# A two-layer trunk with a hierarchical mixture of experts: further blocks taken apart, a third late expert, fillers between routing products

## What is computed

```python
def hierarchical_moe(t, wg, bg, we, be, w1, w3, w2):
    g_sel = jnp.argmax(g_logit, axis=-1)                       # 4 groups
    e_logit = jnp.take_along_axis(e_logit, g_sel[:, None, None], axis=1)[:, 0]
    top_p, top_i = lax.top_k(jax.nn.softmax(e_logit, axis=-1), TOP_K)     # 2 of 8
    top_w = top_p / jnp.sum(top_p, axis=-1, keepdims=True) * g_w
    ...
        hidden = jax.nn.silu(t @ w1_e) * (t @ w3_e)            # 1024 -> 256
        return acc + c_e[:, None] * (hidden @ w2_e), None      # for 32 experts
```

## Time and profile before

| | us |
|---|---|
| median of 3 runs (1046.13 to 1048.80) | 1048.57 |
| the profiled execution | 1048.56 |
| its span | 1046.8 |
| TensorE busy | 970.4 (93%) |
| VectorE / ScalarE / GpSimd busy | 362.8 / 248.2 / 213.4 |
| HBM read / written | 315.38 MB / 22.31 MB |

### The profile page before, as it was taken

One profiled execution on the slowest core, in us unless ns is written; L12 is line 12 of the kernel. 1 busy time (PEld: TensorE's weight loads), 2 busy tenths in 40 slices (PEclk: granted clock), 3 DMA queues, 4 the chain that ended last, 5 costly groups with the idle time before them and its releaser, 6 DMA issues.

```text
span 1046.8 us, 17807 instructions
## 1 busy us (share of the span) xinstructions
PE 970.4 (93%) x6151; PEld 614.8 (59%) x6152; DVE 362.8 (35%) x851; ACT 248.2 (24%) x537; POOL 213.4 (20%) x307
## 2 busy tenths in 40 slices
PE   5999999998998899998989899999998999998896
PEld 3444457545887455555555384877875555555552
DVE  4159493564337111110011370145444222221124
ACT  5110003444334122221221240033132111111112
POOL 1009300110001243332331100000003333333310
PEclk9999999999998899998999999999998999999899
DMA  9984546999715699999999899273646997999996
GB/s 361 307 273 176 198 115 233 315 339 381 293 66 191 228 385 406 406 406 407 407 406 406 320 317 309 81 279 108 223 166 232 389 399 290 407 405 403 404 405 232
DMA packets 129161, 315.95 MB, mean 302 GB/s; under 512 B 28969, under 2 KB 59969, under 8 KB 129076
## 3 DMA queue, kind: packets, MB, share of 16 engines
q1 hardware_dynamic: 113200, 295.98, 75.9%
q0 software_dynamic: 10880, 12.72, 3.6%
q10 hardware_dynamic: 4996, 6.09, 1.6%
HBM read 315.38 MB, written 22.31 MB: 323 GB/s over the span
## 4 chain that ended last, share of the span: by engine, by line
PE 73%; DMA 14%; DVE 5%; issue 3%; SPq 2%; ACT 2%; POOL 0%; POOLq 0%; DVEq 0%
PE ps L1095 17%; PE ps L929 16%; DMA ring<-in_moe_w 9%; PE ps L981 8%; PE ps L1121 8%; PE ps L939 5%; PE ps L883 3%; PE ps L1067 3%; SPq L699 2%; DMA ring<-in_w_mod 1%; PE ps L1248 1%; PE ps L1105 1%; DMA pair_out<-RH,sidx_all 1%; DMA RH<-hrow,sidx_all 1%; PE ps L896 1%
## 5 line engine op out<-in xcount | busy, mean ns | idle before, releaser
L1095 PE MATMUL ps<-ring,RT 128*64 128x256 f32 x2128 | 261.2, 399 | 26.2 <-DMA ring<-in_moe_w 22.6
L1095 PEld LDWEIGHTS ps<-ring,RT 128*64 128x64 f32 x2128 | 164.0, 143 | 98.6 <-issue 29.5
L929 PE MATMUL ps<-RT,ring 128*128 128x512 f32 (+1 forms) x544 | 182.0, 493 | 0.5 <-DVE RT L2244 0.5
L929 PEld LDWEIGHTS ps<-RT,ring 128*128 128x128 f32 x544 | 102.2, 190 | 76.5 <-issue 69.8
L2131 DVE TENSOR_TENSOR RT<-RT,ps 64x256 f32<-64x256 f32 x64 | 27.1, 423 | 275.7 <-ACT RT L1678 275.7
L1121 PE MATMUL ps<-ring,RT 128*64 128x512 f32 x424 | 100.4, 593 | 1.4 <-DVE RT L2137 1.0
L1678 ACT ACTIVATE RT<-ps 64x256 f32<-64x256 f32 x64 | 24.1, 377 | 254.0 <-PE ps L1095 254.0
L2286 DVE SCALAR_TENSOR_TENSOR RAB<-RM,chan,RAB 128x512 f32<-128x512 f32 x120 | 79.7, 746 | 0.0
L2535 POOL DMA_INDIRECT pair_out<-RH,sidx_all x62 | 63.2, 1019 | 54.0 <-POOL sidx_all L2532 54.0
L2511 POOL DMA_INDIRECT RH<-hrow,idx x8 | 8.4, 1046 | 308.5 <-DVE idx L2083 306.7
L2523 POOL DMA_INDIRECT RH<-hrow,sidx_all x56 | 59.0, 1054 | 50.8 <-POOL sidx_all L2520 48.1
(11 more groups left out here) (271 smaller groups left out, 1005.6 us busy)
## 6 DMA issues: line engine op xcount, KB each, us to landing
ring<-in_moe_w SPq DMA_DIRECT2D x358, 512.0 KB, 14.6
ring<-in_w_mod SPq DMA_DIRECT2D x96, 512.0 KB, 9.2
ring<-in_odd_w_in SPq DMA_DIRECT2D x24, 512.0 KB, 9.4
ring<-in_even_w_in SPq DMA_DIRECT2D x20, 512.0 KB, 9.5
ring<-in_even_w_out SPq DMA_DIRECT2D x8, 512.0 KB, 11.4
RAB<-in_moe_w SPq DMA_DIRECT2D x8, 512.0 KB, 7.9
RAB<-pair_out SPq DMA_DIRECT2D x8, 512.0 KB, 5.8
ring<-in_odd_w_out SPq DMA_DIRECT2D x8, 512.0 KB, 3.9
```

The lines of the kernel that those rows point to most:

```text
L929: mm = pe.matmul(bank, w[:, c, P * ft:P * (ft + 1)], moving[:, c, :], start=(c == 0), stop=(c == NCH - 1))
L1095: mm = pe.matmul(bank[CAP * k:CAP * (k + 1), 0:BLK], xt(c), w[k][:, BLK * c:BLK * (c + 1)], start=(c == 0), stop=(c == NCH - 1))
```

## The change

1. TensorE's step is now U(q), the further block's transposes and up products (`more_up`), Dn(q-1), Hd(q), the block's hidden and down products (`more_down`), T(q+2). Only the last further block of an expert is taken apart so; earlier ones of the same expert run whole, in a loop. ScalarE and VectorE follow the same split.
2. `LATE` has three experts. The zeroing moves from before step 0 to before step 28, with `XG[:, 0]` as source. The late rows have three buffers of their own (`XG[:, 0]`, `YS[:, 0]`, `YS[:, 1]`), and the one-hot products of the late experts are interleaved with Dn(31). Their slots are transposed tile by tile, in steps 28 and 29.
3. The choice of two goes by `dve.max` (the eight largest) on the logits and on keys that also hold the expert's place, one tile at a time; tile 0's group choice is a shorter chain.
4. One `warm` product pair between any two blocks of `slot_rows`; in layer 1 eight behind them instead of four; in layer 0 one tile's row transposes take the place of `warm(("lgT", l, 0), 3)`.

```diff
-LATE = (EXPERTS - 2, EXPERTS - 1)
+LATE = (EXPERTS - 3, EXPERTS - 2, EXPERTS - 1)
...
                 mm = rows(out, at_slot[:, (b + 1) % 2, :, :], vs)
                 if b < n_blocks - 2:
                     mm.then_inc(slot_used, 1)
+                if b == 0:
+                    drained(pe, "rank", l)
+                if b < n_blocks - 1:
+                    warm(("rank", l), 1)
...
-                def step(i, q, count, ahead=True):
-
-                    if ahead:
-                        T(*job_after(i, q, 1))
-                    Hd(i, q - 1)
-                    U(i, q)
-                    if isinstance(i, int) and (i, q) == (LAST_GROUP, 1):
-                        pe.wait_ge(late_ready, l + 1)
-                    more(i, q, count)
-                    used(i, q, (0, 1))
-                    Dn(i, q - 1)
-                    used(i, q - 1, (2,))
+                def step(i, q, count, ahead=True, first=False):
+
+                    if not first:
+                        U(i, q)
+                    if isinstance(i, int) and (i, q) == (LAST_GROUP, 1):
+                        late_slots(1, LATE_TILES[1])
+                        pe.wait_ge(late_ready, 2 * l + 2)
+                    more_up(i, q, count)
+                    used(i, q, (0, 1))
+                    if not first:
+                        Dn(i, q - 1)
+                        used(i, q - 1, (2,))
+                    Hd(i, q)
+                    more_down(i, q, count)
                     if ahead:
+                        T(*job_after(i, q, 2))
...
+                    late_added(banks, 1, 0)
+                    Dn(LAST_GROUP, PER_LOOP - 1)
+                    used(LAST_GROUP, PER_LOOP - 1, (2,))
+                    late_added(banks, 1, 1)
+                    late_added(banks, 0, 0)
+                    late_added(banks, 0, 1)
+                    late_added(banks, 1, 2)
+                    first_choices(banks, 1)
+                    late_added(banks, 0, 2)
+                    first_choices(banks, 0)
...
-            drained(pe, "rank", 1)
-            warm(("rank", 1), 4)
+            warm(("rank", 1), 8)
             experts(1)
...
             def two_choices(ts):
 
-                step(dve.tensor_reduce(emax[:, ts], masked[:, ts, :], AX.X, ALU.max))
-                first_of(emax, first_choice, ts)
...
+                for t in range(ts.start, ts.stop):
+                    step(dve.max(best[:, t, :], masked[:, t, :]))
+                    step(dve.scalar_tensor_tensor(out=in_two[:, t, :], in0=masked[:, t, :], scalar=best[:, t, 1:2],
+                                                  in1=const[:, C_PLACE:C_PLACE + EXPERTS], op0=ALU.is_ge, op1=ALU.mult))
+                    step(dve.scalar_tensor_tensor(out=cand[:, t, :], in0=masked[:, t, :], scalar=best[:, t, 0:1],
+                                                  in1=in_two[:, t, :], op0=ALU.is_ge, op1=ALU.add))
+                    step(dve.max(best_keys[:, t, :], cand[:, t, :]))
+                    step(dve.tensor_tensor(choices[:, :, t, :], cand[:, t, :].unsqueeze(1).broadcast_to([P, 2, EXPERTS]),
+                                           best_keys[:, t, 0:2].unsqueeze(2).broadcast_to([P, 2, EXPERTS]), ALU.is_equal))
...
                 ahead(0, 0, counts[0])
-                late_zeros()
                 for q in range(PER_LOOP):
...
                 counts = extra_counts(pool, l, LAST_GROUP)
+                late_zeros()
                 for q in range(PER_LOOP):
```

More of the change, by code:

```diff
@@ L282 @@
 PEELED = 3
-LATE = (EXPERTS - 2, EXPERTS - 1)
+LATE = (EXPERTS - 3, EXPERTS - 2, EXPERTS - 1)
 LATE_TILES = (1, 0)
+SCATTERED = [sum(e % 2 == b for e in range(LATE[0])) for b in (0, 1)]
 LATE_BANKS = {(1, 0): 0, (1, 1): 1, (0, 0): 2, (0, 1): 4}
@@ L450, in trunk @@
         rexp = temp(980, 5, 4)
-        gmax, emax, emax2, least, gsum = [temp(1000 + 4 * i, 4) for i in range(5)]
+        gmax, least, gsum = [temp(1000 + 4 * i, 4) for i in range(3)]
         rank_of = temp(1020, 8)
@@ L998, in norm_and_logits @@
                 transpose_tile(k, 0)
-                warm(("lgT", l, 0), 3)
+                for t in early[1:]:
+                    tile_rows(l, t)
+                if not early:
+                    warm(("lgT", l, 0), 3)
                 feature_logits(l, 0)
                 token_logits(l, 0)
-                for t in (early + (1,))[1:] + (0,):
+                for t in (1, 0) if early else (0,):
                     tile_rows(l, t)
@@ L1125, in down, with block_up @@
                     return mm
-                def more(i, q, count):
+                def block_up(w):
+                    bank = ps[:, 7, :]
+                    done = pe.snap(extras)
+                    pe.reg_add(extras, extras, 1)
+                    x = pe.snap(extras)
+                    pe.wait_ge(x_y_ready, done)
+                    pe.sem_inc(pe_passed, 1)
+                    pe.wait_ge(x_gathered, x * 16)
+                    for j in range(4):
+                        mm = pe.transpose(bank[:, P * j:P * (j + 1)], XGX[:, j:512:4], ident)
+                    mm.then_inc(x_xT_full, 1)
+                    pe.wait_ge(x_xT_ready, x)
+                    up(w, lambda c: XTX[:, c % 4, c // 4, :], bank).then_inc(x_up_full, 1)
@@ L1207, in experts @@
                 c = extra_counts(pe, l, 0)
-                more(0, 0, c[0])
-                used(0, 0, (0, 1))
-                for q in range(1, PER_LOOP):
-                    step(0, q, c[q])
+                for q in range(PER_LOOP):
+                    step(0, q, c[q], first=(q == 0))
                 for i in range(1, PEELED):
@@ L1707, in one, with copy_late_y @@
-                def one(i, q, count, ahead=True):
-                    if ahead:
-                        copy_xT(*job_after(i, q, 1))
-                    silu(i, q)
-                    more(q, count)
-                    if l == 0:
-                        copy_y(i, q - 1)
+                def copy_late_y(e):
+                    act.wait_ge(y_full, n0 + LATE[e] + 1)
+                    if e == 0:
+                        act.wait_ge(late_zeroed, 16 * len(LATE))
+                    else:
+                        act.wait_ge(scattered[e - 1], (LAST_GROUP * 2 + 2 - e + l * SCATTERED[e - 1]) * 16)
+                    act.activation(late_rows[e], ps[:, 5 + LATE[e] % 2, :], ACT.Copy).then_inc(y_ready, 1)
@@ new lines, in more_result, with one @@
+                def more_result(count):
+                    if l == 0:
+                        with act.If(count > 0):
+                            block_result()
+                def one(i, q, count, ahead=True, first=False):
+                    if not first:
+                        silu(i, q)
+                    if isinstance(i, int) and (i, q) == (LAST_GROUP, 1):
+                        late_slots(1, LATE_TILES[1])
+                    more_up(count)
+                    if l == 0 and not first:
+                        if isinstance(i, int) and PER_LOOP * i + q - 1 in LATE:
+                            copy_late_y(LATE.index(PER_LOOP * i + q - 1))
+                        else:
+                            copy_y(i, q - 1)
+                    more_result(count)
+                    if ahead:
+                        copy_xT(*job_after(i, q, 2))
@@ L1719, in experts @@
                 c = extra_counts(act, l, 0)
-                more(0, c[0])
-                for q in range(1, PER_LOOP):
-                    one(0, q, c[q])
+                for q in range(PER_LOOP):
+                    one(0, q, c[q], first=(q == 0))
                 with act.Fori(1, LAST_GROUP) as i:
@@ new lines, in one @@
+                def one(i, q, count, first=False):
+                    if not first:
+                        hidden(i, q)
+                    more_hidden(count)
+                    if l == 1 and not first:
+                        if isinstance(i, int) and PER_LOOP * i + q - 1 in LATE:
+                            gated_late_y(LATE.index(PER_LOOP * i + q - 1))
+                        else:
+                            gated_y(i, q - 1)
+                    copy_hT(i, q)
+                    more_result(count)
```

288 lines of the change are left out of this document (155 added, 133 removed).

## The result

The changed kernel takes 1059.59 us (median of 5 runs, 1055.97 to 1061.13) against 1048.57 us of the kernel before (5 runs in all, 1046.04 to 1052.67): a ratio of 1.0102, 95% interval 1.0069 to 1.0136. It is slower by about 11 us. The forecast of 1043.2 us and its range up to 1051 are both missed, and so is the sign. The profiled execution of the changed kernel is its fastest, 1055.97 us with a span of 1054.2; the profiled one of before took 1048.56 us with 1046.8.

A forecast was written before the change was run, and what follows sets the result against it. Weight transfers at about 404 GB/s bound the expert stages, held up early by a full ring. Layer 0's -5.0 us (-4.7 + 0.5 - 0.8) and layer 1's -0.3 took 1048.56 to 1043.3, called 1043.2; range 1037 to 1051.

The forecast's parts named there:

- The step that failed: Each step's two skips of further-block code (two bodies, second branch behind Hd) cost nothing, hidden behind U and Dn.
- the rule: A taken branch with target outside the two fetched pages stalls until the page comes; sum then near the third rival's time.
- the third rival: Steps behind the further block each have a 0.73 us sequencer gap, losing 5 us: about 1048; chance 0.12.
- (a): Layer 0 routing: VectorE's choice for the last tile shrinks from 3.66 to about 2.3 us; net 1.1 us earlier.
- (b): Layer 0 routing: seven filler pairs between slot products cost +2.8 us, with the clock falling and returning after about two blocks.
- the first rival: TensorE's clock does not fall during routing, so both layers' streams come sooner: about 1039.5 us; chance 0.16.
- the second rival: Clock stays at half until U(0) in both layers and fillers lengthen the routing: 1054 us, slower; chance 0.13.
- (e) to (h): Layer 0's further block: earlier rows -1.4, full-clock up products -1.7, filled wait -1.0, release before hidden/down products 3.6 us.
- The booking of -4.7 for the release: Layer 0: earlier release of ring slots around the further block moves the weight stream by -4.7 us, between 4.1 and 6.6.
- The tail of layer 0: End of layer 0: the read back is there in time, VectorE's four halves end the stage as before: -0.8 us.
- Layer 1 was to end 0.3 us earlier: Layer 1's total over choice, fillers, release, further block, zeroing and tail: -0.3 us.
- three signs of being wrong: Layer 0's first transposes after about 343 us, a regular step over 6.5 us, or saturated stretches losing their 404 GB/s.

The follow-up runs named there:

- e2_before_two: Kernel before plus a second, never-run copy of the further block's body on TensorE alone; 1057.37 us, ratio 1.0104.
- e3: Changed kernel without the filler products between the slot products; 1056.99 us, ratio 1.0110.
- e9: Changed kernel with the second body copy kept only on TensorE, in the hardware loop's groups (experts 12 to 27); 1046.22 us, ratio 0.9982.
- e10: Changed kernel with the second body copy kept only on TensorE, in the first twelve experts' written-out code; 1060.58 us, ratio 1.0125.
- e11: Changed kernel without the steps' second copies, but twelve dead copies in one place ahead of the first step, behind one never-true condition; 1060.60 us, ratio 1.0142.
- e5: Changed kernel with further blocks in one loop whose later turns first finish the block before, so up products stand once per step; 1046.20 us, ratio 0.9998.
- e8: e5 with the further block in one piece again, hidden and down products directly behind its up products; 1048.98 us, ratio 1.0000.
- e7: Changed kernel with the inner loop for several further blocks left out on TensorE alone; 1046.50 us, ratio 0.9976.
- e14: e12 measured once more, as the pair of e13 on the same chip; 1044.95 us, ratio 0.9980.
- e13: e12 with the routing lines of the kernel before; 1044.77 us, ratio 0.9973.
- e12: e5 with the third expert's row transposes ahead of the hidden transposes again in each layer's first step; 1046.57 us, ratio 0.9991.

## Why the prediction was wrong

**The step that failed** is the sentence "so I cost it at nothing; the cover is U's 3.67 us for the first skip and Dn's 1.9 for the second". I looked for the cost of a skip where the skipped body was half as long, found 0.0 us, and carried that over. That row could not show the price of bringing the code, since it was just hidden there. What the runs showed in its place is a wait for code: 11 us for dead copies alone (e2_before_two), in gaps that end when a block of code has come. In the changed kernel, e2, e3, e9, e10 and e11 every issue gap of 0.6 us or more between U(0) and U(31) ends 2.3 to 2.9 us after the start of a packet of the instruction queue; in the runs without second copies on TensorE no gap there is above 0.6. The weights make no difference to this: it is 2.5 us with the DMA engines full (392.68) and 2.9 with none at work (813.77).

The margin was small and unseen. A copy of the body is 6.6 KB (e2), so an estimate from the counts of products (46 in a step, 46 in the body) is 13 KB for a step with one body and 20 KB with two. At 6.37 us a step, a packet's worth of code would then last 7.9 us in the kernel before and 5.3 in the changed one. Measured, the packets start 7.9 us apart on average before (376 to 456 us) and 6.1 in the changed kernel (378 to 451). Why most of them still come in time and some do not is argued: a packet holds two and a half skipped bodies, so where TensorE jumps over most of one it wants the next sooner than the 2.3 to 2.9 us.

I did name the rule, as one by which the sum would end near the third rival's 1048 us. The sign was right and the size was not: I had priced a gap by the 0.73 us ahead of U(0), which was not a gap of this kind: it stands ahead of layer 0's U(0) in every run, with or without second copies, and no packet of code starts in the 4 us before it. Those that came are 0.3 to 2.8 us each and sum to some 7 us in each layer's stage. It deserved a rival of its own, since the order of instructions showed the code growing and nothing bounded the price from above.

**The other terms**, by the changed kernel's trace:

- (a) The choice of the last tile runs from 328.11 to 330.67 us and takes 2.56 us, against 3.66 before and 2.3 forecast. A maximum of eight costs 0.20 us (I took 0.19), but steps with a scalar from memory cost 0.25 on 128x32, and the other three tiles ended 0.7 us later:

```profile
329.38 0.19 DVE L2120 MAX8 RM<-RM 128x8 f32<-128x32 f32 x1
329.60 0.25 DVE L2121 SCALAR_TENSOR_TENSOR RM<-RM,const 128x32 f32<-128x32 f32 x1
329.89 0.25 DVE L2123 SCALAR_TENSOR_TENSOR RM<-RM 128x32 f32<-128x32 f32 x1
330.18 0.20 DVE L2125 MAX8 RM<-RM 128x8 f32<-128x32 f32 x1
330.41 0.22 DVE L2126 TENSOR_TENSOR RM<-RM 128x64 f32<-128x64 f32 x1
330.67 0.29 DVE L2133 TENSOR_TENSOR RM<-RM 128x128 f16<-128x128 f32 x1
```

  The choice ends 0.35 us earlier (331.02 before), not 1.1.
- (b) The clock did not fall in this execution (the granted clock was 1.00 over 322 to 346 us), so the first rival's condition held. In e9's the slot products and fillers ran at the 1.2 GHz level, the second rival's condition, with 1.72 us a turn instead of 1.00 and U(0) at 348.5 us. Both occur, and this alone moves the start of the stage by 4.7 us. That execution of e9 is its slowest, 1051.55 us against a median of 1046.22, close to what the second rival booked. The other four executions of the changed kernel show a granted clock of 0.980 to 0.985 over the whole, against 0.991 in the profiled one, so part of their 3 to 5 us may be this; it is not shown, since one execution has a trace.

```profile
338.06 1.22 PE L902 MATMUL ps<-const 128*128 128x256 f32 x2
339.21 0.64 PE L1040 MATMUL ps<-PR,RM 128*64 128x64 f16 x16
339.77 1.22 PE L902 MATMUL ps<-const 128*128 128x256 f32 x2
340.93 0.64 PE L1040 MATMUL ps<-PR,RM 128*64 128x64 f16 x16
```

- (e) to (h) Right up to U(2): the block's transposes wait for no rows, its up products take 3.67 us, Dn(0) follows at once, and U(2) starts 3.7 us earlier (367.61 to 363.90; forecast 4.1). In layer 1 the block's transposes still wait for rows, 1.15 us.

```profile
353.52 0.75 PE L1150 MATMUL ps<-const,RH 128*128 128x128 f32 x4
354.95 3.67 PE L1108 MATMUL ps<-ring,RT 128*64 128x256 f32 x32 [0.69 <-ACT RT L1754]
358.46 1.89 PE L1134 MATMUL ps<-ring,RT 128*64 128x512 f32 x8
...
363.90 3.67 PE L1108 MATMUL ps<-ring,RT 128*64 128x256 f32 x32
```

- The booking of -4.7 for the release was too large. In e5, which has all of the change but the dead copy, layer 0's last up products U(31) start 2.8 us earlier than before (579.73 to 576.95), where the release less the zeroing was to give 4.2. e8 says why: what a release wins in a stretch in which TensorE then paces the stream counts by TensorE's own 1.4 us, not by the 3 to 4 us of the empty stretch.
- The tail of layer 0 came as forecast in kind, and more of it: the four products behind the read back have no idle ahead and take 1.98 us instead of 3.60, and from U(31) to the end of VectorE's last half e5 takes 21.8 us against 23.4 before, 1.6 less where 0.8 was booked.
- Layer 1 was to end 0.3 us earlier. The terms written out for it (+0.5 for the release, -0.6 for the block, +0.5 for the zeroing, 0 for the tail) do not give -0.3 but between -0.1 and +0.4, a slip too small to matter. From its first to its last up products e5 takes 223.1 us, e7 223.4, e14 222.8, e13 221.3, e12 220.9 and before 221.9. Why these differ is open: clock and landings vary between executions by as much.
- None of the three signs of being wrong came: the first transposes of layer 0 start at 342.33 us, a regular step takes 6.37 us, and the stretch of 408 to 580 us has its 404 GB/s. They watched the terms of the sum, and the step that failed stood outside it.

Without the dead copies the change is worth 0 to 2.5 us (0.9976 to 0.9998), and the forecast had 5.3 (0.9949). The third rival came nearest: gaps of the sequencer, spent where TensorE paces the stream. It priced each at 0.73 us and took 5 us from a gain of 5.3; the gaps were up to 2.8 us, and the gain they were taken from was smaller.

## What to carry to other kernels

When an edit copies a body under a condition, count its code even if it never runs: what an engine skips must still be fetched or jumped over, and it costs first in code that is written out and run once, where the engine sets the pace. Compare the instruction queue's packets of both kernels, and look for idle time labelled issue where the engine sets the pace; a loop's code came once, and its later turns waited for none. If the general case needs a second turn of the same work, fold it into one loop with a condition (e5_shared: the loss of 1% gone, nothing else changed); the lowest ratio here, e13_old_routing's 0.9973 (e7's 0.9976 and e14's 0.9980 are within its noise), is this fold with the old routing and the rows first.

## What the runs showed of the hardware

- Dead code under a condition that is never true cost 11 us in a kernel of 1048 (e2_before_two), in gaps of 0.5 to 3.2 us, some in the middle of unbroken products.
- TensorE goes on 2.3 to 2.9 us after the start of the packet of code (16.4 KB) that it waits for, with the DMA engines full (share 1.03 over 389 to 393 us in the changed kernel) as with none at work (0.00 over 812 to 813 us in e11).
- One far skip cost 9.0 us in layer 0, three such packets one after the other, and 2.4 and 2.7 us in layer 1, one packet each.
- During such a stall the granted clock fell (0.58 over 349 to 356 us in e11), and U(1) behind it took 5.04 us instead of 3.67.
- Code in a hardware loop was fetched once for four turns: e9 has no packet of the instruction queue between 460.4 and 563.3 us.
